# Layer 1's feed-forward blocks 3+4 and 6+7: seven half-depth products a pair in place of eight, in a two-layer decoder trunk

## The reference

```
mod = silu(c) @ w_ada + b_ada                       # six vectors of 1024 a layer
...
h = _rmsnorm(x, g_pre_ffn) * (1.0 + sc2) + sh2
f = (jax.nn.silu(h @ w_gate) * (h @ w_up)) @ w_down # w_gate, w_up 1024 x 2816; w_down 2816 x 1024
return x + gt2 * _rmsnorm(f, g_post_ffn)
```

## Time and profile before

| | |
|---|---|
| median of 3 runs | 846.04 us (845.91 to 846.12) |
| the profiled execution | 845.91 us, span 844.1 us from its first to its last instruction |
| PE busy | 835.2 us, 99% |
| DVE busy | 646.4 us, 77% |
| ACT busy | 446.3 us, 53% |
| granted TensorE clock | 0.999 of full speed |

### The profile page before, as it was taken

One profiled execution on the slowest core, in us unless ns is written; L12 is line 12 of the kernel. 1 busy time (PEld: TensorE's weight loads), 2 busy tenths in 40 slices (PEclk: granted clock), 3 DMA queues, 4 the chain that ended last, 5 costly groups with the idle time before them and its releaser, 6 DMA issues.

```text
span 844.1 us, 11561 instructions
## 1 busy us (share of the span) xinstructions
PE 835.2 (99%) x4155; PEld 694.2 (82%) x4155; DVE 646.4 (77%) x1150; ACT 446.3 (53%) x723; POOL 122.2 (14%) x92
## 2 busy tenths in 40 slices
PE   8999999999999999999999999999999999999997
PEld 6877888888888888888888788888888888888885
DVE  5798889888788776786689899898787866545743
ACT  5665555565757434433476556565565745334422
POOL 5500300301210021030420040040040000000300
PEclk9999999999999999999999999999999999999999
DMA  8996676576417788787438756766642576664611
GB/s 342 415 360 233 217 257 252 203 270 224 144 57 299 290 282 324 251 305 278 183 120 310 284 204 219 276 214 243 221 150 100 198 276 213 247 236 177 223 51 51
DMA packets 34795, 194.10 MB, mean 230 GB/s; under 512 B 4273, under 2 KB 4529, under 8 KB 17714
## 3 DMA queue, kind: packets, MB, share of 16 engines
q1 hardware_dynamic: 33410, 189.64, 61.4%
q0 software_dynamic: 1328, 3.71, 1.3%
HBM read 192.29 MB, written 1.05 MB: 229 GB/s over the span
## 4 chain that ended last, share of the span: by engine, by line
PE 95%; DMA 3%; DVE 1%; SPq 0%; issue 0%; DVEq 0%; ACT 0%
PE ps L1483 26%; PE ps L1485 26%; PE ps L1484 26%; PE ps L1596 4%; DMA wide_t<-scale_first 3%; PE ps L1660 2%; PE ps L1520 1%; PE ps L1521 1%; PE ps L1527 1%; PE ps L1681 1%; PE ps L1682 1%; PE ps L1659 1%; PE ps L1680 1%; PE ps L1642 1%; PE ps L1612 1%; PE ps L1834 0%
## 5 line engine op out<-in xcount | busy, mean ns | idle before, releaser
L1006 DVE TENSOR_TENSOR w_lo<-raw,w_hi 128x2048 fp32r<-128x2048 f32 (+2 forms) x128 | 294.8, 2309 | 60.2 <-ACT w_hi L654 59.1
L1483 PE MATMUL ps<-w_hi,t_hi 128*128 128x512 f32 (+2 forms) x776 | 306.9, 395 | 1.0 <-DVE w_lo L1006 0.9
L1485 PE MATMUL ps<-w_hi,t_lo 128*128 128x512 f32 (+2 forms) x776 | 300.0, 387 | 0.0
L1484 PE MATMUL ps<-w_lo,t_hi 128*128 128x512 f32 (+2 forms) x776 | 299.4, 386 | 0.0
L654 ACT ACTIVATE w_hi<-raw 128x2048 fp32r<-128x2048 f32 (+2 forms) x130 | 244.8, 1885 | 25.5 <-DMA raw<-w_stream 16.9
L1483 PEld LDWEIGHTS ps<-w_hi,t_hi 128*128 128x128 f32 x776 | 145.8, 188 | 32.1 <-DVE w_lo L1006 1.9
L1485 PEld LDWEIGHTS ps<-w_hi,t_lo 128*128 128x128 f32 x776 | 145.7, 188 | 30.2
L1484 PEld LDWEIGHTS ps<-w_lo,t_hi 128*128 128x128 f32 x776 | 146.0, 188 | 27.6
L555 POOL PARTITION_ALL_REDUCE wide_t<-wide_t x20 | 80.0, 3998 | 555.7 <-DVE wide_t L1034 554.8
L1034 DVE SCALAR_TENSOR_TENSOR wide_t<-ada,cs,wide_t 128x1024 f32<-128x1024 f32 x80 | 110.3, 1379 | 1.0 <-DMA ada<-w_ada 0.7
L966 ACT ACTIVATE relu<-ps 128x256 f32<-128x256 f32 x44 | 17.0, 386 | 147.4 <-PE ps L1485 147.4
(11 more groups left out here) (226 smaller groups left out, 911.4 us busy)
## 6 DMA issues: line engine op xcount, KB each, us to landing
raw<-w_stream SPq DMA_DIRECT2D x126, 1024.0 KB, 5.2
ada<-w_ada SPq DMA_DIRECT2D x80, 512.0 KB, 5.6
wide_t<-gains POOLq DMA_DIRECT2D x7, 512.0 KB, 4.6
raw<-w_stream SPq DMA_DIRECT2D x4, 656.0 KB, 7.4
mixed<-scale_first SPq DMA_DIRECT2D x2, 1024.0 KB, 9.7
wide_t<-shift_first SPq DMA_DIRECT2D x4, 512.0 KB, 10.5
wide_t<-scale_first SPq DMA_DIRECT2D x2, 1024.0 KB, 12.7
ada<-shift_first SPq DMA_DIRECT2D x4, 512.0 KB, 12.5
```

The lines of the kernel that those rows point to most:

```text
L1006: nc.vector.tensor_tensor(w_lo[:, U % RING, a:n], src[:, a:n], w_hi[:, U % RING, a:n].bitcast(F32), ALU.subtract).then_inc(s_lo, 1)
L1483: nc.tensor.matmul(dst, hi, w_h, start=first, stop=False)
L1484: nc.tensor.matmul(dst, hi, w_l, start=False, stop=False)
L1485: return nc.tensor.matmul(dst, lo, w_h, start=False, stop=last)
```

## The change

In layer 1, blocks 3 and 4 are projected upwards together, and so are 6 and 7 (`TWINS = ((), (3, 6))`). With token tiles 0 and 1, upper and lower rows of the weights, and block `j` and `j+1`, an upward projection of a pair is a product of 2 x 2 by 2 x 2 parts. It was eight half-depth products (12 matmuls each); it is now seven (`twin_up`, `seventh`), as in Strassen's scheme in Winograd's form, on sums of the parts:

- Sums of tokens, once for both pairs: `add_tokens`, five chained VectorE operations at the head of step 1; `sums_hi` on ScalarE in step 1; `sums_low` on VectorE at the head of step 2.
- Sums of weights, four a pair (`add_weights`), in place in the `mixed` buffer, which serves as a fourth raw buffer, and in one raw buffer, each 128 x 2048 on VectorE, behind the low split of the seventh 0, 1 and 3.
- A pair has seven upward units of `w_hi` and `w_lo` in place of four, so three more splits on each of ScalarE and VectorE. What is loaded stays the same: four upward units a pair.
- The products are put together with one ScalarE copy and five VectorE additions of 128 x 512 a pair (`add_products`), some of which the next product's bank or the gating waits for.
- TensorE in a pair: the seven products, `down_chunk(j-1, 0)`, `turn_m(j, 0)`, `turn_m(j, 1)`, `down_chunk(j-1, 1)`, `down_chunk(j, 0)`, `turn_m(j+1, 0)`, `turn_m(j+1, 1)`, `down_chunk(j, 1)`.
- The pieces of the gate table move: steps 0, 1, 2 and 5 keep one, and step 8 has four. The three before were in steps 3, 4, 6 and 7.

The core of the diff (units are now found by name; `BASE[l] + u` stands for `l * UNITS + u`):

```diff
+TWINS = ((), (3, 6))
+TWIN_SUMS = (1, 4, 3, 6)
...
-    return (1, 1, 1, 1, 1, 1, 1, 1, 0, 0, 0), (9,)
+    return (1, 1, 1, 0, 0, 1, 0, 0, 4, 0, 0), (9,)
...
+                n = len(freed)
+                loads.append([("sum", twin_no(l, j), l, up_at(j + 1)), ("raw", n, l, up_at(j)), ("raw", n + 1, l, up_at(j) + 1)])
+                freed += [U + 4, U + 5, U + 4]
...
+            def twin_hi(l, j):
+                split_hi(l, ahead[0])
+                wait_twin(act, l, j, 0)
+                nc.scalar.activation(twin_a, ps[:, QKT, :], ACT.Copy).then_inc(s_kept, 1)
+                for u in behind[:4]:
+                    split_hi(l, u)
+                act.wait_ge(s_twin, 5 * p + 4)
+                silu(l, j, 0, twin_c[:, 0:256], -1.0)
+                silu(l, j, 1, twin_b[:, 0:256], -1.0)
+                split_hi(l, behind[4])
...
+                    if j == sums_step(l):
+                        act.wait_ge(s_sums, sums_no(l))
+                        nc.scalar.activation(sums_hi[:, :, :], sums[:, :, :], ACT.Copy).then_inc(s_sums_hi, 1)
...
+            def add_weights(U, e):
+                if e == 0:
+                    dve.wait_ge(upper[1], upper[2])
+                    nc.vector.tensor_tensor(w_sum, w_sum, upper[0], ALU.add).then_inc(s_w_sum, 1)
+                    dve.wait_ge(lower[1], lower[2])
+                    nc.vector.tensor_tensor(upper[0], upper[0], lower[0], ALU.add).then_inc(s_w_sum, 1)
+                else:
+                    nc.vector.tensor_tensor(w_sum, w_sum, (lower if e == 1 else corner)[0], ALU.add).then_inc(s_w_sum, 1)
...
+            def twin_lo(l, j):
+                split_lo(l, ahead[0])
+                split_lo(l, behind[0])
+                split_lo(l, behind[1])
+                add_products(l, j, twin_a, twin_a, SCO, 3, 1)
+                add_products(l, j, twin_b, twin_a, PTB, 1, 2)
+                split_lo(l, behind[2])
+                add_products(l, j, twin_b, twin_b, OUT, 4, 3)
+                split_lo(l, behind[3])
+                add_products(l, j, twin_c, twin_a, PTB, 5, 4)
+                gate_m(l, j, 0, twin_c[:, up], -1.0)
+                gate_m(l, j, 1, twin_b[:, up], -1.0)
+                add_products(l, j, twin_a, twin_a, OUT, 6, 5)
+                split_lo(l, behind[4])
+                m_lo_split(l, j, 0)
...
+                    if j == sums_step(l):
+                        add_tokens(l)
+                    elif j == sums_step(l) + 1:
+                        sums_low(l)
...
+            def twin_up(l, j):
+                pe.wait_ge(s_m, before + 1)
+                seventh(0, QKT, t_hi, t_lo, 0, 0)
+                pe.wait_ge(s_sums_lo, sums_no(l))
+                pe.wait_ge(s_act_lo, l * N_SPLIT + turn_no("m", 2 * (j - 1)))
+                seventh(1, PTB, sums_hi, sums_lo, 1, 1)
+                pe.wait_ge(s_kept, p + 1)
+                seventh(2, QKT, t_hi, t_lo, 1, 0, first=False)
+                pe.wait_ge(s_m, before + 2)
+                seventh(3, SCO, sums_hi, sums_lo, 0, 0)
...
+                seventh(4, OUT, sums_hi, sums_lo, 0, 1)
+                pe.wait_ge(s_twin, 5 * p + 2)
+                seventh(5, PTB, sums_hi, sums_lo, 1, 0, first=False)
+                pe.wait_ge(s_twin, 5 * p + 3)
+                seventh(6, OUT, t_hi, t_lo, 1, 1, first=False)
```

More of the change, by code:

```diff
@@ L347, in hybrid_decoder_trunk, with stored @@
         shift_at = (wide_t[:, 0, :], wide_t[:, 1, :], ada[:, 0, :], ada[:, 1, :])
-        def raw_no(U):
-            return U - sum(u < U for u in SPARE)
-        def raw_at(U):
[L355 to L363, removed]
+        def stored(kind, n):
+            if kind == "spare":
+                return scale_at[n], s_spare[n], 16
+            if kind == "sum":
+                return w_sum, s_sum_in, 16 * (n + 1)
+            return raw[:, n % RAW, :], s_raw[n % RAW], 16 * (n // RAW + 1)
+        def raw_at(U):
+            return stored(*SOURCE[U])
         cs_wide = qkT[:, 0:KT * 32].rearrange("p (k n) -> p k n", k=KT)
@@ L418, in hybrid_decoder_trunk @@
         used_units = [[chunk_units(l, c)[0] for c in range(N_CHUNK) if c != 1] + [OUT_UNIT + i for i in range(KT // 2 - 1)]
-                      + sorted([up_unit(j) for j in range(N_FF)] + [down_unit(j) for j in range(N_FF - 1)])
+                      + [u for u, (kind, *at) in enumerate(LAYER_NAMES[l])
+                         if kind == "twin" or kind == "up" and at[1] == 0 or kind == "down" and at[0] < N_FF - 1]
                       for l in range(DEPTH)]
@@ L949, in _ @@
                 border(l, True)
-                for j in range(N_FF):
-                    ahead, behind = up_splits(j)
+                for j, *both in ffn_steps(l):
+                    if both:
+                        twin_hi(l, j)
+                        continue
+                    ahead, behind = up_splits(l, j)
                     for u in ahead[:1]:
@@ new lines, in sums_low, with add_products @@
+            def sums_low(l):
+                dve.wait_ge(s_sums_hi, sums_no(l))
+                nc.vector.tensor_tensor(sums_lo[:, :, :], sums[:, :, :], sums_hi[:, :, :].bitcast(F32),
+                                        ALU.subtract).then_inc(s_sums_lo, 1)
+            def add_products(l, j, to, of, bank, after, count):
+                p = twin_no(l, j)
+                wait_twin(dve, l, j, after)
+                if count == 1:
+                    dve.wait_ge(s_kept, p + 1)
+                else:
+                    dve.wait_ge(s_twin, 5 * p + count - 1)
+                nc.vector.tensor_tensor(to, of, ps[:, bank, :], ALU.add).then_inc(s_twin, 1)
@@ L1441, in _ @@
                 border(l, True)
-                for j in range(N_FF):
-                    ahead, behind = up_splits(j)
+                for j, *both in ffn_steps(l):
+                    if both:
+                        twin_lo(l, j)
+                        continue
+                    ahead, behind = up_splits(l, j)
                     many = ffn_pieces(l)[0][j]
+                    if j == sums_step(l):
+                        add_tokens(l)
+                    elif j == sums_step(l) + 1:
+                        sums_low(l)
                     for u in ahead[:1]:
@@ L1490, in hi_then_lo @@
                     for k in range(KT):
[L1491 removed]
+                        U, at = BASE[l] + unit(k), (k % 4) * cols
                         if part == "hi":
@@ L1898, in down_chunk @@
                     pe.wait_ge(s_xup, xup_no(l, True, t))
-                down(l, down_unit(j), t, mix_at(m_hi, t_hi, j % 2), mix_at(m_lo, t_lo, j % 2), j == 0, j == N_FF - 1)
+                down(l, down_unit(l, j), t, mix_at(m_hi, t_hi, j % 2), mix_at(m_lo, t_lo, j % 2), j == 0, j == N_FF - 1)
             first_phase()
@@ L1966, in _ @@
                 turn_m(l, 0, 0)
-                for j in range(1, N_FF):
+                for j, *both in ffn_steps(l)[1:]:
+                    if both:
+                        twin_up(l, j)
+                        continue
                     up(l, j, 0)
```

246 lines of the change are left out of this document (197 added, 49 removed).

## The result

| | before | after |
|---|---|---|
| median of the runs | 845.97 us (845.40 to 846.12) | 851.04 us (850.93 to 851.37) |
| ratio to before, 95% interval | | 1.0062 (1.0044 to 1.0079) |
| span of the profiled execution | 844.1 us | 849.2 us |
| granted TensorE clock | 0.999 | 0.995 |

The account below looks back on a forecast made before the run. TensorE was taken to bound the kernel: 24 removed matmuls save 5.4 us, and waits of 4.3, 4.4 and 3.9 us for VectorE make +7.2, taken as 7.1. Forecast 853.0 us, range 849.5 to 857.2.

Parts of the forecast that it names:

- What bounds the kernel: Layer 1's feed-forward part: TensorE bounds it; each removed matmul is worth 0.227 us, 24 together 5.4 us.
- First wait: Step 1: token sums on VectorE stand ahead of `m(1, 0)`, so `down_chunk(0, 1)` starts late; 4.3 us lost (4.1 to 4.7).
- Second wait: Step 2: VectorE's queue with the first weight sums delays `m(2, 0)`; 4.4 us lost on top (3.8 to 5).
- The clock: Rival: TensorE's clock falls in the long waits, 2 us lost a fall; 855 for one, 857 for both; chance 0.22.
- Inside the pairs: Pairs 3+4 and 6+7: waits before product 6 (1.3 and 1.0) and `down_chunk` (0.8 each); together 3.9 us (2 to 8).
- The 0.8 before each `down_chunk(j, 0)`: In each pair: the low split of `m`, behind two silus and two splits on ScalarE, costs 0.8 us.
- Hidden work: Extra high splits fit ScalarE's idle time; the later gate table is covered by some 6 us; nothing lost.
- Sum: Whole kernel: -5.4 + 4.3 + 4.4 + 3.9 = +7.2 us, step by step +7.0, taken as 7.1; forecast 853.0 us.
- the likeliest case: The forecast itself, without the rivals: 853.0 us, its own range 850.8 to 855.5, chance 0.62.
- The signs: Listed trace observations, in steps 1 and 2, the pairs, step 5 and the gate table, showing the forecast right or wrong.
- those named as right: Two PE idles of some 4 us, products 2.72 us apart, short pair waits, gapless VectorE some 17 us, block 8 near 789.
- those named as wrong: Gapless PE in step 1, token sums far from 5.2 us, step 5 or table wait, clock below 1.00, pair wait over 3.

Follow-up runs that it names:

- the sums moved: The changed kernel with the token sums moved from ahead of step 1's `m`s to behind `m(1, 1)`: 853.32 us, ratio 1.0086.
- one filler: The changed kernel with 15 unread matmuls of 512 columns on TensorE ahead of `turn_m(1, 0)`: 851.72 us, ratio 1.0073.
- both fillers: The changed kernel with 15 unread matmuls of 512 columns ahead of each late turn, of `m(1, 0)` and `m(2, 0)`: 851.43 us, ratio 1.0064.
- the first pair alone: The changed kernel with only blocks 3 and 4 as a pair, without pair 6+7: 853.01 us, ratio 1.0083.
- the third addition first: The changed kernel with VectorE's third product addition ahead of the low split of `down(j-1)`'s unit in both pairs: 852.01 us, ratio 1.0072.
- pairs 4+5 and 7+8: The changed kernel with these pairs, token sums heading step 2, ScalarE's split ahead of `sums_hi`, four table pieces in step 9: 843.83 us, ratio 0.9978.
- one kernel above: The changed kernel with pairs 4+5 and 8+9, token sums heading step 2, ScalarE's split ahead of `sums_hi`, table pieces moved: 851.85 us, ratio 1.0070.
- the last run above: The kernel with pairs 4+5 and 7+8, with both `m` of the step before a pair ahead of its first split: 848.03 us, ratio 1.0026.

## Why the prediction was right or wrong

- **What bounds the kernel**: right. At the upper level of the clock the matmuls of a dozen stand 0.227 to 0.231 us apart on average, also in the pairs, and the stretch from pair 3+4's start to the end is shorter by the 5.4 us of 24 matmuls less the 2.3 lost in the pairs.
- **First wait**: 4.3 forecast, 4.2 measured. The five sums took 5.1 us with their hand-overs (676.25 to 681.35), for 5.15 and 0.1.
- **Second wait**: 4.4 forecast, 4.0 measured (8.2 - 4.2). The prediction took it as what is left up to `m(2, 0)`, whose time it worked out from VectorE's queue; that is the step that held. The time of `m(2, 0)` was forecast at 703.65 and was 703.15. But only 1.6 of the 4.0 is a wait; 2.2 is the low clock behind the first one and 0.2 the slower turns. How the loss divides before `m(2, 0)` makes no difference to the sum: in all six kernels that make both kinds of sums ahead of pair 3+4 (the changed one and those with the sums moved, one filler, both fillers, the first pair alone and the third addition first), that turn came at 703.2 to 704.0, whatever TensorE did before.
- **The clock**, a rival at 0.22 priced as 2 us on top: the fall did happen, in the first wait and not in the second. Its price was about right (2.2 us and 0.4 in the turns, for 2) and its place in the sum wrong: it was added to the 853.0, and what it took was slack until the second wait. Where the clock fell was luck: in the second wait, as in the run of the third addition, it would have made the pair begin about 1.6 us later. In the last wait before the pair it costs, as with the token sums moved (853.32), the filler in the first wait alone (851.72) and in the run of the third addition. The Trainium skill ("TensorE: Matmul & The Clock Gate", "What's actually happening") has the fall after idleness and the return under sustained work; the trace agrees on both.
- **Inside the pairs**: 3.9 forecast, 2.3 measured; this is the term that was mis-sized. Product 6 waited 1.0 us and 0.5 by the distance of starts (723.08 and 772.13 were due), for 1.3 and 1.0; another 0.8, in the two pairs together, went in restarts and in matmuls some thousandths of a us wider apart. The 0.8 before each `down_chunk(j, 0)` did not come: with product 6 late, TensorE came to it late as well. It came when product 6 was on time (0.2 and 0.6 with the third addition first). I added two waits of which the first swallows the second in this kernel; that isn't so everywhere, for with pairs 4+5 and 7+8 a late product 6 (0.7) was followed by a wait for a low part of `m` (0.4).
- **Hidden work**: the table was ready in time (VectorE finished it at 824.5, and `m(10, 0)` came at 827.1), and step 5 had no wait: right. The table had 2.6 us to spare where some 6 were forecast, since GpSimd's sum took 8.5 and not 7.48, and the finishing step stood behind a split (821.03).
- **Sum**: the terms made +7.2 and the spans differ by 5.1. Of the 2.1 too much, 1.6 lie in the pairs and 0.5 in the first two waits. The time of 851.04 lies in the range given, and just inside the likeliest case's own of 850.8 to 855.5, which is narrower than the bounds of the terms make it: added up they give 850.4 to 858.2.
- **The signs**: of those named as right came the first wait of some 4 us, seven products 2.7 us apart, the wait of product 6 and VectorE's 17.5 us without a gap. The second stretch was 1.6 us and not 4, no `down_chunk` waited, and block 8 began at 787.43, not near 789. Of those named as wrong one came, the clock below 1.00. So the likeliest case was right in VectorE's queue and in what removed matmuls are worth, but not in its clock, nor in its waits behind product 6.

What stays open: why the third addition first is 0.5 us slower with pairs 4+5 and 7+8 (the intervals overlap, and the two profiled executions, 844.23 and 844.66, stand the other way round), how much of the gain with those pairs is due to the place of the sums alone, and how often the clock falls in the second wait, of which I have single traces.

## What to carry to other kernels

Two waits of one engine for one queue are not summed: compute when the queue delivers the last thing wanted, and what the waiting engine loses before that, a low clock too, is free as long as the engine is back by then. Work for an engine that is busy half the time is hidden only if it lies where its queue has time before the next delivery: here a kernel with the same sums was 5 us slower than before with them ahead of block 3, and 2 us faster one block later (with ScalarE's order and the table changed as well). That move was worth more than the reorderings that I tried (the token sums behind `m(1, 1)`, the third addition, the two `m` ahead of a split), none of which gained, and where the work is moved to has to be free of GpSimd as well. A pair that carries such sums broke even at best here; the gain came from the second pair, for which they are already made.

## What the runs showed of the hardware

- **VectorE's splits slow down beside GpSimd's sum over partitions**: 2.29 us alone, 4.33 beside it; in one kernel above it made TensorE wait for 4.9 us. The Trainium skill ("SBUF — State Buffer", "Who interferes with whom") says that a VectorE instruction with two SBUF inputs contends with a GpSimd instruction that reads SBUF, and that the pair of ports they share is an exclusive lock. The trace agrees that they collide (a split reads two SBUF tiles); the split of 4.33 ran across the end of the reduction at 798.44, and from durations alone I can't tell a lock from a sharing. Which began first did matter: in the changed kernel a split at 808.20 began just ahead of the sum at 808.37 and kept its 2.28 us, and the sum took 8.53, for 6.56 in the last run above, where no split lay beside it. The additions with an operand in PSUM, at 799.51, were at their usual length, but the reduction was over by then.
- **The clock's fall isn't at a fixed distance from the last matmul.** It came 2.2 us after the end of the last one in the changed kernel (678.40 to 680.64), and 3.9 us with the first pair alone (678.36 to 682.26). With the third addition first it came only at about 682.75, when matmuls had been running again for 0.5 us. Once down it stayed for 6.8, 3.4 and 3.4 us, so the dozen behind the same wait lost 2.2 us in the first, 1.4 in the second (682.95 to 687.05) and 1.7 in the third (682.85 to 687.23).
